# Layer attention rewritten: query blocks in pairs, probabilities scaled before they are turned, gates finished in the projections

## The reference

```python
q, k, v, up, uf, g = split_proj(h @ w_in[l])        # 8 query heads, 2 key and value heads, gate of 2048
q = apply_axial_rope(rmsnorm_2(q...)); k = ...
def attend(qg, keys, vals):
    s = jnp.einsum('bqkgd,bskd->bkgqs', qg, keys) * (HEAD_DIM ** -0.5)
    p = jax.nn.softmax(s, axis=-1)
    return jnp.einsum('bkgqs,bskd->bqkgd', p, vals)
# latent queries: 768 keys (context and latent); context queries (first layer only): the 256 context keys
mixed = jnp.concatenate([att, multiscale_pool(...), fourier_mix(...)], axis=-1)
out = (mixed * jax.nn.silu(g)) @ w_out
```

## Time and profile before

| | us |
|---|---|
| median of 3 runs | 3105.42 (3098.38 to 3107.28) |
| profiled execution | 3112.03 |
| its span | 3110.3 |
| TensorE busy | 2862.3, 92% |
| VectorE busy | 1596.3, 51% |
| ScalarE busy | 956.8, 31% |
| POOL busy | 450.5, 14% |
| mean granted TensorE clock | 0.961 of full speed |
| layer 0 attention, from the first score to VectorE's last low part | 166.9 |
| the same in layer 1 | 138.0 |

### The profile page before, as it was taken

How to read it: one execution, slowest core, us unless ns; L and a number is a source line. 1 busy time by engine, 2 the same in 40 slices (tenths; PEclk the granted TensorE clock), 3 DMA queues, 4 the chain that set the end, 5 groups by cost and what they waited for, 6 DMA issues and landing times. The chain is left out here.

```text
span 3110.3 us, 35771 instructions
## 1 busy us (share of the span) xinstructions
PE 2862.3 (92%) x13746; PEld 2186.1 (70%) x13746; DVE 1596.3 (51%) x2138; ACT 956.8 (31%) x1601; POOL 450.5 (14%) x609
## 2 busy tenths in 40 slices
PE   7899999988448999999999998899989999989897
PEld 5666666676226867888888875488878877865685
DVE  6678778776554443125533337622243374547434
ACT  4444444443333333122211113311132232223221
POOL 2544444425101021000000001000010000001000
PEclk9999999999669999999999999999999999999998
DMA  5577777762123233233323332222213344431421
GB/s 196 189 303 291 289 299 285 302 241 100 48 88 108 95 126 125 75 115 132 115 100 133 120 136 69 102 76 93 89 77 118 138 163 145 164 135 62 156 95 54
DMA packets 111684, 447.15 MB, mean 144 GB/s; under 512 B 11440, under 2 KB 19760, under 8 KB 76208
## 3 DMA queue, kind: packets, MB, share of 16 engines
q1 hardware_dynamic: 111536, 445.16, 39.1%
HBM read 375.25 MB, written 69.86 MB: 143 GB/s over the span
## 5 line engine op out<-in xcount | busy, mean ns | idle before, releaser
L2524 PE MATMUL ps<-h_hi,w_hi 128*128 128x512 f32 x1600 | 576.9, 361 | 0.0
L2525 PE MATMUL ps<-h_lo,w_hi 128*128 128x512 f32 x1600 | 565.1, 353 | 0.0
L2526 PE MATMUL ps<-h_hi,w_lo 128*128 128x512 f32 x1600 | 561.4, 351 | 0.0
L384 PE MATMUL ps<-h_hi,w_hi 128*128 128x512 f32 (+1 forms) x1152 | 413.6, 359 | 37.7 <-DVE w_lo L343 37.7
L385 PE MATMUL ps<-h_lo,w_hi 128*128 128x512 f32 (+1 forms) x1152 | 412.6, 358 | 0.0
L386 PE MATMUL ps<-h_hi,w_lo 128*128 128x512 f32 (+1 forms) x1152 | 410.6, 356 | 0.0
L2524 PEld LDWEIGHTS ps<-h_hi,w_hi 128*128 128x128 f32 x1600 | 301.9, 189 | 49.8 <-issue 6.2
L2525 PEld LDWEIGHTS ps<-h_lo,w_hi 128*128 128x128 f32 x1600 | 301.7, 189 | 46.5 <-issue 6.2
L2526 PEld LDWEIGHTS ps<-h_hi,w_lo 128*128 128x128 f32 x1600 | 300.7, 188 | 43.6
L2305 DVE TENSOR_TENSOR w_lo<-raw,w_hi 128x2048 fp32r<-128x2048 f32 x64 | 146.4, 2288 | 310.6 <-ACT w_hi L2216 310.5
L2170 ACT ACTIVATE xw<-ps 128x512 f32<-128x512 f32 x112 | 53.9, 518 | 794.1 <-PE ps L2526 753.6
(11 more groups left out here) (370 smaller groups left out, 4672.8 us busy)
## 6 DMA issues: line engine op xcount, KB each, us to landing
raw<-w_in SPq DMA_DIRECT2D x112, 1024.0 KB, 5.1
raw<-ada_w SPq DMA_DIRECT2D x96, 1024.0 KB, 8.5
raw<-w_out SPq DMA_DIRECT2D x48, 1024.0 KB, 5.0
proj<-xw SPq DMA_DIRECT2D x60, 384.0 KB, 2.5
xw<-proj SPq DMA_DIRECT2D x70, 256.0 KB, 3.2
xw<-proj SPq DMA_DIRECT2D x46, 384.0 KB, 3.2
xw<-resid SPq DMA_DIRECT2D x8, 1536.0 KB, 12.7
proj<-wide SPq DMA_DIRECT2D x32, 256.0 KB, 11.1
```

Source lines behind the costliest of these rows:

```text
L384: pe.matmul(a_[q], wh, h_hi[:, h0 + k, lo:hi], start=k == 0, stop=False)
L2524: pe.matmul(a_[q], wh, h_hi[:, k, a:b], start=k == 0, stop=False)
L2525: pe.matmul(a_[q], wh, h_lo[:, k, a:b], start=False, stop=False)
L2526: ins = pe.matmul(a_[q], wl, h_hi[:, k, a:b], start=False, stop=k == KC - 1)
```

## The change

`layer_attention` replaces `attention(..., mixed=True)` for both layers; `attention` loses its `mixed` branches and is left to the memory attention. Units of a head are ordered latent, latent, context, context, latent, latent in layer 0 and are taken in pairs of equal kind. The probabilities are multiplied by the reciprocal of their row sum in place, by VectorE, before they are turned; there are three tiles of them. ScalarE reads out the turned blocks, VectorE no longer does. The values product is made for a pair (256 queries), in one of two banks, and its result, high and low part follow pair by pair; the low parts are POOL's. The diagonals and the matmul with ones are gone. The gates are finished in `projections`: ScalarE takes the tanh as it reads the tile out, and VectorE multiplies, `gate_out`, in the next tile's turn. The layers' weight loads keep their place; key and value loads of the second group move to head 1.

```diff
+        def layer_attention(l, then):
+            latent = [(b * P, 0, W) for b in range(TB)]
+            units = latent if width == T else latent[0:2] + [(T, T, CT), (T + P, T, CT)] + latent[2:4]
...
+                @block.sync
+                    for i in range(HEADS2):
+                        if i:
+                            if i > 1:
+                                sp.wait_ge(s_ready.h, s_ready.at(nu * (i - 1)))
+                            sp.dma_start(q_sb[i % 2]...)
+                        if i == 1:
+                            sp.dma_start(k_sb[1], proj2[9]); sp.wait_ge(m3.h, m3.at(1)); sp.dma_start(v_t[1], proj2[11])
...
+                        if i > 1:
+                            sp.wait_ge(res_lo.h, res_lo.at(pairs * (i - 1)))
+                        sp.dma_start(g_sb[i % 2]...)
+                        sp.wait_ge(mixd_lo.h, mixd_lo.at(i))
+                        sp.dma_start(mix_sb...)
+                        if i == 0:
+                            prime(sp, then)
...
+                    def scores(g):
+                        pe.wait_ge(exp_done.h, exp_done.at(g - 1))
...
+                    def turned(g):
+                        pe.wait_ge(p_ready.h, p_ready.at(g + 1))
+                        pe.wait_ge(t_out.h, t_out.at(g))
...
+                    def weighted(pr):
+                        pe.wait_ge(t_out.h, t_out.at(2 * pr + 2))
+                        pe.wait_ge(res_done.h, res_done.at(pr - 1))
+                        for c in range(nch):
+                            ins = pe.matmul(o_ps[pr % 2], v_sb[:, vc, :], pt[pr % 2][:, c, :], start=c == 0, stop=c == nch - 1)
+                    scores(0); scores(1); values(0)
+                    for g in range(total):
+                        if g + 2 < total:
+                            scores(g + 2)
+                        turned(g)
+                        if g and g % 2 == 0:
+                            weighted(g // 2 - 1)
+                        if g == v_unit:
+                            pe.wait_ge(t_out.h, t_out.at(g + 1))
+                            values(1)
+                    weighted(total // 2 - 1)
...
+                @block.gpsimd
+                    for g in range(total):
+                        if g % 2 and g > 4:
+                            low((g - 5) // 2)
+                        if g % nu == 2:
+                            mixed(g // nu)
...
+                @block.scalar
+                    exp(0); exp(1); v_out(0)
+                    for g in range(total):
+                        read_out(g)
+                        if g == v_unit:
+                            v_out(1)
+                        if g + 2 < total:
+                            exp(g + 2)
+                        if g % nu == 2:
+                            mixed(g // nu)
+                        if g % 2 and g > 2:
+                            result_high((g - 3) // 2)
...
+                    def normalise(g):
+                        dve.wait_ge(exp_done.h, exp_done.at(g + 1))
+                        dve.reciprocal(rs[g % ring], sm[g % ring])
+                        dve.wait_ge(st.sem, st.now)
+                        dve.tensor_scalar(p_, p_, rs[g % ring], None, ALU.mult).then_inc(p_ready.h, 1)
+                    def result(pr):
+                        dve.wait_ge(o_ready.h, o_ready.at(pr + 1))
+                        dve.scalar_tensor_tensor(x, o_ps[pr % 2], 0.5, x, ALU.mult, ALU.mult).then_inc(res_done.h, 1)
+                    for g in range(total):
+                        if g + 2 < total:
+                            peak(g + 2)
+                        if g % 2 and g > 2:
+                            result((g - 3) // 2)
+                        if g + 2 < total:
+                            normalise(g + 2)
...
@@ projections, ScalarE's read_out and VectorE
+                        gate = isinstance(n, int) and n >= gates            # gates = 28
+                            ins = act.activation(stage[par][:, a:b], a_, ACT.Tanh, scale=0.5) if gate else \
+                                act.activation(stage[par][:, a:b], a_, ACT.Copy)
+                        ins.then_inc(gate_tanh.h if gate else staged.h, 1)
...
+                    def gate_out(n):
+                        dve.wait_ge(gate_tanh.h, gate_tanh.at(n - gates + 1))
+                        for q, (a_, (a, b)) in enumerate(zip(accs(par, w_), w_)):
+                            ins = dve.scalar_tensor_tensor(t_, t_, 1.0, a_, ALU.add, ALU.mult)
+                            ins.then_inc(staged.h if q == len(w_) - 1 else st.step(), 1)
...
                                 dve.tensor_tensor(w_lo[:, j % 2, :], raw[:, j, :], w_hi[:, j % 2, :].bitcast(F32), ALU.subtract)
+                                if kind == "mix" and n > gates:
+                                    gate_out(n - 1)
                                 if kind == "mix":
                                     mix_turn(4 * i + j - 2)
+                    gate_out(IN2 - 1)
```

More of the change, by code:

```diff
@@ L202, in program @@
         odd_copied, shifted = count("odd_copied"), count("shifted")
+        v_copied, res_done, res_hi, res_lo, gate_tanh = (count(n) for n in (
+            "v_copied", "res_done", "res_hi", "res_lo", "gate_tanh"))
         row_out = [count(f"row_out{i}") for i in range(4)]
@@ L1332, in glu, with attention @@
             four_st.base += 32
-        def attention(heads, group, units, nkeys, qcols, q_src, k_src, v_src, g_src, chunk0, then, mixed=False):
+        def attention(heads, group, units, nkeys, qcols, q_src, k_src, v_src, g_src, chunk0, then):
             nch = nkeys // P
@@ L1346, in take @@
                 return xw[:, at[0] - size:at[0]]
[L1348 to L1353, removed]
+            th, res, g_sb = take(qcols), take(qcols), take(qcols)
+            q_sb, k_sb, v_t = [take(qcols)], [take(nkeys)], take(nkeys)
             q_sb += [wide[:, 0:qcols]]
@@ L1359, in attention @@
             pt = take(nch * qcols).rearrange("p (c q) -> p c q", c=nch)
-            mix_sb = take(qcols) if mixed else None
             s_ps, t_ps, o_ps = [psum[0], psum[1]], psum[2], psum[3]
@@ L1375, in _ @@
                             sp.wait_ge(s_ready.h, s_ready.at(nu * (i - 1)))
-                        if i or not mixed:
-                            sp.dma_start(q_sb[i % 2], q_src(i)).then_inc(loaded[i % 2].h, 16)
-                        if i % group == 0 and (i or not mixed):
+                        sp.dma_start(q_sb[i % 2], q_src(i)).then_inc(loaded[i % 2].h, 16)
+                        if i % group == 0:
                             if kv > 1:
@@ L2015, in projections @@
             p_gate = cnt
+            gates = 28
             p_th = [sums[g % 2] for g in range(4)]
@@ L2299, in _ @@
                         dve.wait_ge(st.sem, st.now)
+                    def gate_out(n):
+                        par, w_ = n % 2, parts[-1][2]
+                        dve.wait_ge(gate_tanh.h, gate_tanh.at(n - gates + 1))
+                        for q, (a_, (a, b)) in enumerate(zip(accs(par, w_), w_)):
+                            t_ = stage[par][:, a:b]
+                            ins = dve.scalar_tensor_tensor(t_, t_, 1.0, a_, ALU.add, ALU.mult)
+                            ins.then_inc(staged.h if q == len(w_) - 1 else st.step(), 1)
                     for iters, n0, segs, kind in parts:
@@ L2603, in projections @@
                          (rot_done, 11), (rot_read, 10), (q_done, 10), (up_in, 64 * len(tok)), (uf_in, 64), (cnt_in, 64),
-                         (pgate_in, 64), (fgate_in, 64), (pool_st, 64), (four_st, 64), (chan_done, 4), (odd_copied, 4), (y_copied, 4),
+                         (pgate_in, 64), (fgate_in, 64), (gate_tanh, IN2 - gates), (pool_st, 64), (four_st, 64), (chan_done, 4), (odd_copied, 4), (y_copied, 4),
                          (four_done, 4), (pooled, 4), (pool_done, 4), (p_tanh, 4), (f_tanh, 4), (pool_out, 4), (four_out, 4)):
@@ L2660, in program @@
             projections(l)
-            units = [(b * P, 0, W) for b in range(TB)]
-            if not last:
-                units[0:0] = [(T, T, CT)]
-                units[5:5] = [(T + P, T, CT)]
-            width = T if last else W
-            def gate(h):
-                return row(proj2, h + 28)[:, 0:width]
-            def query(h):
-                return row(proj2, h)[:, 0:width]
-            attention(HEADS2, HEADS2 // KV2, units, W, width, query, lambda kv: proj2[8 + kv], lambda kv: proj2[10 + kv],
-                      gate, 0, lambda n: row(w_out2, n + 16 * l), mixed=True)
+            layer_attention(l, lambda n: row(w_out2, n + 16 * l))
             out_projection(w_out2, 16 * l, [(0, T)] if last else both, l, then=None if last else lambda n: row(w_in2, n + IN2))
```

152 lines of the change are left out of this document (130 added, 22 removed).

## The result

| | before | changed |
|---|---|---|
| median, us | 3106.35 (3098.38 to 3110.4, 4 runs) | 3062.99 (3058.82 to 3065.49, 4 runs) |
| ratio, 95% interval | | 0.9862 (0.9849 to 0.9876) |
| profiled execution, its span | 3112.03, 3110.3 | 3058.82, 3057.0 |

A forecast was written before the change was run, and what follows sets the result against it. TensorE was taken to bound every stage, attention less tightly. Gains of 28.4 us in layer 0 and 15.0 in layer 1 sum to 43.4, from a median of 3105.4 to 3062; range 3050 to 3080.

The forecast's parts named there:

- Step 1: TensorE's attention work: row sums go, products in pairs cost nothing more; 15.4 us a layer-0 head, 13.2 in layer 1.
- Step 2: Serial chain of maximum, exp and scaling on VectorE and ScalarE: 2.92 us a latent unit, 15.0 a layer-0 head, 11.7 layer 1.
- The bound above, 0.95: Upper bound for VectorE's 768-wide scaling, from a read-out of the same width; the forecast took 0.56 us.
- Step 3: How TensorE's order meshes with the chain: layer-0 heads slip to 16.0 us, layer 1 runs at 13.2.
- a slip: In layer 0, a head's first transposes wait for a scaling that ends late: 0.6 us a head.
- stalls nothing: The single turned bank costs no wait, as ScalarE's 0.80 us read-out runs during TensorE's next score, 1.30.
- Step 4: Lengths of the two attention stretches: layer 0 takes 137.4 us, gaining 28.4 with its later start; layer 1 gains 15.0.
- The low clock, taken at 2 us: Term in layer 0's stretch for a low clock at its start, as before the change: 2 us.
- The 1 us for head 1's queries: Term in layer 0's stretch: TensorE waits 1 us for the load of head 1's queries.
- Step 5: Gate multiplies in the projections: seven of eight a layer cost nothing; the last delays attention by 1.1 and 0.7 us.
- Step 6: POOL's low parts, 4.4 and 3.0 us a head, cost nothing because they start when the scaling is over.
- Rival C: Attention look-ahead fails, one unit in flight: layer 0 loses 118 us, layer 1 90, time 3270; chance 0.03.

The follow-up runs named there:

- the early maximum: Changed kernel with head 1's queries loaded first and, in layer 0, VectorE's maximum of the next head's first unit one place earlier: 3052.75 us, 0.982.
- the late product: On top of the early maximum, layer 0's context-pair values product moved to just ahead of the next head's first transposes: 3053.28 us, 0.983.
- the last experiment: Changed kernel with the last gate tile's multiply in each layer's projections on 8 columns only, the rest unfinished: 3060.01 us, 0.9857.

## Why the prediction was right, step by step

Step 1 (TensorE's work per head) stands and carries the result. In the steady heads a layer-0 head has 15.2 us of work (four scores 5.18, two short ones 0.87, transposes 2.62 and 0.44, products 5.18 and 0.87), predicted 15.4; a layer-1 head 12.97, predicted 13.2, with TensorE busy throughout. The small excess was in the transposes, 0.69 from a row that included a restart, against 0.65. The product with ones, put back, cost its 1.29 and 0.87 a head.

Step 2 (the chain): 2.94 measured, 2.92 predicted, but two errors cancel: the scaling takes 0.62 and not 0.56, so that its successor starts 0.54 after it, not 0.48; and from the small multiply to the reciprocal it is 1.21 (1867.58 to 1868.79), not 1.26. The bound above, 0.95, was near the truth of another instruction form (1.02), which cost 10 us.

Step 3 (the mesh): a slip of 0.8 and not 0.6 a head, so 16.0 as predicted, since work was 0.2 less. The waits stand where that step had them, at the exp and the scaling of a head's start. But the slip isn't the chain's alone: with the early maximum (15.84) the single turned tile holds TensorE at the same place, against the step's "stalls nothing", and with the late product (15.69) it is the chain again, with one scaling slowed beside POOL.

Step 4 (the stretches): layer 0 took 141.33 and not 137.4. Two terms were too small. The low clock, taken at 2 us, cost 4.3: the first eight score matmuls took 5.25 instead of 2.66 (as in the last experiment), and the last product 4.51 instead of 2.83, which it takes in half of the profiles. And the last head was counted as pure work, though there are no scores of a next head to cover the chain: waits of 0.52, 0.87 and 0.95 are 2.3. The 1 us for head 1's queries didn't arise; together 3.6 of the 3.9. Layer 1 gained 16.95 (predicted 15.0): heads were 0.2 shorter, 1.8 in all, and the 0.7 that it was to start later is not seen between the stretches. That the wait for the queries was 6.70 and not 8 is no gain: the load ends it, 16.96 us after the stretch's start, where the forecast had 16.5.

Step 5 (the gates): hand-overs 1.06 and 0.72 longer (1.98 to 3.04 and 1.71 to 2.43), predicted 1.1 and 0.7; the projections hide the rest. The kernel before, TensorE at both starts:

```profile
1839.52 1.96 PE L1417 MATMUL ps<-xw 128*128 128x256 f32 x6 [1.98 <-PEq L2034]
...
2765.48 2.82 PE L1417 MATMUL ps<-xw 128*128 128x512 f32 x8 [1.71 <-PEq L2034]
```

Finished in the heads, the gates cost 7.3 us more, hand-overs included.

Step 6 (POOL) was right in its price and wrong in its reason. Two of the three low parts of a layer-0 head do meet a scaling:

```profile
1855.93 0.62 DVE L1735 TENSOR_SCALAR xw<-xw,stat 128x768 f32<-128x768 f32 x1
```

```profile
1856.08 1.05 POOL L1661 TENSOR_TENSOR h_lo<-xw,h_hi 128x256 fp32r<-128x256 f32 x1 [4.81 <-ACT h_hi L1699]
```

But the scaling begins first, and it is POOL that takes 1.05 instead of 0.73, where nothing waits for it. By the Trainium skill (SBUF — State Buffer, section "SBUF: two separate sides") the one of the two that starts first has the shared ports for its whole instruction. The traces agree on who pays, in both directions: 0.62 and 1.05 here, 0.72 and 0.93 with the late product, 1.81 and 1.65 with the gates in the heads. So a scaling is not held whenever it meets a low part, as this step read the rule, but only when the low part is first. And the delays, 0.32, 0.31 and 0.69, are 0.13 to 0.19 shorter than the overlaps that were left, so in these rows the second is not held quite to the end of the first.

The sum of 43.4 us is the 43.36 between the medians, whose ratio leaves 38.5 to 46.9 open. By the profiles it is 25.6 less the later start of 1.1, 16.95, and 2.3 behind layer 1 that I can't place: 43.8. So the exact hit is luck, the size is not: 3.9 too much in layer 0, against 1.95 and 2.3 too little behind it. Rival C, the only one with a slower kernel, had no sign: TensorE is busy 15.6 of 16.0 us. What no run takes back alone is the scaling ahead of the turn, without the read-outs' move, and the products in pairs.

Three variants beat the changed kernel and their medians don't tell them apart (3053.7, 3052.8 and 3053.3); all have head 1's queries first, which is 8.4 us, and that is nearly all of their gain over it.

## What to carry to other kernels

Where one engine bounds a pipeline, price its work by differences of starts, and then find for each instruction of the others what stands ahead of it in its own queue: here a copy that by length fits into idle time cost 38 us behind a maximum and a result, and a low part some 10 us because a load stood behind it in a DMA queue. A load that the next head needs goes ahead of bulk loads. In these traces POOL's low parts were free where VectorE's scaling started first, and slowed it where they did; a shift of 0.4 us turned that round.

## What was not expected of the hardware

The granted clock at the start of a stretch depends on more than the wait ahead of it: eight score matmuls took 5.46 after 3.03 to 3.07 us in eight profiles, 4.46, 4.20 and 4.19 after 3.03 and 3.04 in three others, 4.51 after 1.98 and 2.82 after 2.18. What decides between them no run here separates. POOL's 256-column subtract took 0.72 alone and 1.05 beside a scaling that began 0.15 us before it. The delay fell on whichever of the two began second.
